# Second mixer with its differential branch first, bias loads spread over the experts, and one tile split ahead of the group copies

## The chip, the cores and the metric

The program runs on one core of one Trainium2 chip, in one launch. The metric is the device time of that core in microseconds (us). The core's engines run side by side and meet at semaphores: TensorE (PE, matmuls), VectorE (DVE), ScalarE (ACT), GpSimd (POOL) and SyncE (SP), which issues the weight loads.

## The reference

A sequence of 256 tokens of width 1024 passes two blocks in float32, each of two layers. The first block has a hybrid mixer and 32 experts, of which each token takes two out of one group of eight. The second block, which the larger part of the change is in, has per layer one input projection, four attention branches side by side, an output projection and an MLP:

```python
h = rms_norm_2(x, norm1_g[l])
proj = h @ w_in[l]                                   # 256 x 2400
(a_cq, a_ckv, a_kr, b_q, b_k, b_v, c_q, c_k, c_v, d_q, d_k, d_v) = jnp.split(proj, splits, axis=-1)
y_a = mla_mixer(...)    # A: latent; q = rms(cq) @ w_uq, k = rms(ckv) @ w_uk, v = rms(ckv) @ w_uv, rope, 4 heads
y_b = diff_mixer(...)   # B: differential; 4 heads x 2 softmaxes, w = p0 - lam * p1, rope
y_c = swa_mixer(...)    # C: sliding window with sinks, rope
y_d = na_mixer(...)     # D: neighbourhood, with the bias table na_rpb added to the scores
mix = jnp.concatenate([rms_norm_2(y_a, out_g_mla[l]), y_b, rms_norm_2(y_c, ...), rms_norm_2(y_d, ...)], axis=-1)
x = x + mix @ w_out[l]
h = rms_norm_2(x, norm2_g[l])
x = x + jnp.square(jax.nn.relu(h @ w_up[l])) @ w_down[l]
```

## The kernel before

**Weights.** Every weight matrix is cut into tiles of at most 1 MB (128 x 2048 float32). `tile()` lists them in one order, and SP loads them in that order into a ring of four slots. A slot is free when the tile four places back has been consumed. For nearly all tiles this means split: ACT writes the rounded high part of the tile into one of three `spl` buffers (`act_hi`, L356), DVE writes the rest (`dve_lo`, L365), and TensorE multiplies high and low parts in three passes. SP waits for the DVE part of the tile four back (`slot_free`). One tile per layer of the second block, the latent weights `("mla", l)`, is not split: TensorE reads it out of the ring, and its slot comes free only when the last of its matmuls (w_uv, L1666) is done.

**Experts** (`act_moe`, `dve_moe`, `pe_moe`, 32 per layer). Expert e brings three tiles, gate, up and down. TensorE does gate and up of e (L1112, 48 matmuls), down of e-1 (L1126, 12), and a turn (L1136). ACT does the silu (L1188), a copy (L1197) and three tile splits per expert. After each eight experts (a group) DVE scales the group's sum (L1300), ACT copies it (L1205), POOL and DVE finish it, and TensorE scatters it (L1148). In layer 1, at expert 12, ACT also issues eight small DMAs for the bias of branch D (`act_na_bias`, L1809).

**Second mixer** (`pe_mix2`, `act_mix2`, `dve_mix2`, `pool_mix2`). The input projection is six column blocks, n = 0 to 5, whose columns `IN2` lists. Its results go to four PSUM banks in turn (`in2_bank`). Attention is cut into 20 units, `UNITS` (4 of A, 8 of B, 4 of C, 4 of D), dealt out to three lanes, each with a bank of its own. A unit is three TensorE steps, scores (L1608), transposes of the probabilities (L1617) and the product with v (L1623), with a softmax by DVE and ACT between the first two and a copy by ACT (L1747) between the last two. `pe_misc2` and its counterparts hold the latent prologue (L1639 to L1666), the rope permutations and the end of each branch (`fin2`: a norm, transposes L1697, yT). The output projection (L1588) takes one tile of w_out per branch, in the order A, B, C, D, in two halves each, and adds all in PSUM.

**Order.** Each engine runs its instructions in the order written. In the mixer it is set by strings of digits, `ORDER`: 0 is the projections and splits, 1 to 3 the lanes, 4 the prologue and ends, 5 the eviction of the projection. `steps` takes one step of the lane that each digit names. Nothing moves at run time: an engine whose next instruction waits stands still, with all that is behind it.

## Time and profile before

| | |
|---|---|
| runs | 1802.02, 1809.95, 1810.55 us, median 1809.95 |
| profiled execution | 1809.67 us, of which the profile's span is 1807.4 us |
| busy, share of the span | PE 91%, DVE 65%, ACT 51%, POOL 4% |
| chain that ended last | PE 77%, DVE 10%, ACT 6%, DMA 5% |
| experts of layer 0 and of layer 1, TensorE's first gate matmul to the last down matmul | 284 to 573 us, 794 to 1098 us |
| second mixer, first projection matmul to the last output tile | 1107.7 to 1262.6 us, 1454.3 to 1609.8 us |
| MLP after it | to 1444 us, to the end |

The stage bounds are read from where L1112, L1126, L1560 and L1588 start and end in the timeline. Busy time is the sum of an engine's instructions. A wait in brackets in a row stands in front of its instruction and names what ended it.

### The profile page before, as it was taken

What the parts mean: (1) busy time and instruction counts of PE and PEld (TensorE: products, weight loads), DVE (VectorE), ACT (ScalarE), POOL (GpSimd) and SP (SyncE); (2) the same over time, 40 slices, a digit from 0 to 9 for tenths busy, and PEclk for the clock granted to TensorE, in tenths of its full rate; (3) what the DMA queues carried; (4) which work ended last, traced back from release to release, by engine and by line L of the source; (5) the groups of instructions that cost most, each with busy time, mean ns of one, the idle gap of its engine ahead of it and who ended that gap; (6) DMA issues with size and microseconds to landing.
All of it is one profiled execution on the core that took longest, in us unless ns stands there. A gap on an engine that the chain in (4) does not pass through costs nothing.

```text
span 1807.4 us, 24692 instructions
## 1 busy us (share of the span) xinstructions
PE 1651.7 (91%) x10344; PEld 1417.6 (78%) x10344; DVE 1169.6 (65%) x1311; ACT 922.3 (51%) x1128; POOL 80.5 (4%) x68
## 2 busy tenths in 40 slices
PE   4999868999998999679979998998999999989997
PEld 2676658988987687579878898786899878769996
DVE  1545466988997545759868897584555457645554
ACT  2443136777776453357757775453544445444442
POOL 0110000000000100000000002100000030000000
PEclk8999878999998999889989999996999999889999
DMA  9757244999987765229888994531456516315551
GB/s 344 273 216 261 99 175 147 372 345 347 369 340 271 279 226 201 99 73 374 344 275 332 342 360 122 169 117 62 146 189 205 171 42 195 103 47 190 191 195 65
DMA packets 132241, 392.06 MB, mean 217 GB/s; under 512 B 23200, under 2 KB 36384, under 8 KB 107552
## 3 DMA queue, kind: packets, MB, share of 16 engines
q1 hardware_dynamic: 125008, 386.11, 59.9%
q10 hardware_dynamic: 7120, 4.33, 1.0%
q8 instruction: 84, 1.38, 0.3%
q14 instruction: 29, 0.24, 0.0%
HBM read 389.37 MB, written 1.05 MB: 216 GB/s over the span
## 4 chain that ended last, share of the span: by engine, by line
PE 77%; DVE 10%; ACT 6%; DMA 5%; issue 1%; ACTq 1%; SPq 1%; POOL 0%; POOLq 0%; DVEq 0%
PE ps L1112 15%; PE ps L458 11%; PE ps L2057 10%; PE ps L1126 8%; PE ps L438 5%; DVE spl L365 4%; PE ps L1560 4%; ACT spl L356 3%; PE ps L1588 3%; PE ps L1608 2%; PE ps L500 2%; PE ps L1623 2%; DMA ring<-in_w_ada 2%; PE ps L1538 2%; PE ps L517 1%; PE ps L622 1%
## 5 line engine op out<-in xcount | busy, mean ns | idle before, releaser
L365 DVE TENSOR_TENSOR spl<-ring,spl 128x2048 fp32r<-128x2048 f32 (+2 forms) x318 | 722.0, 2274 | 275.5 <-ACT spl L356 274.4
L356 ACT ACTIVATE spl<-ring 128x2048 fp32r<-128x2048 f32 (+2 forms) x318 | 602.5, 1897 | 306.5 <-PE ps L458 105.3
L1112 PE MATMUL ps<-spl,ur 128*128 128x256 f32 x3072 | 373.6, 282 | 12.1 <-DVE spl L365 11.2
L1112 PEld LDWEIGHTS ps<-spl,ur 128*128 128x128 f32 x3072 | 362.7, 192 | 12.7 <-DVE spl L365 11.5
L458 PE MATMUL ps<-hh,spl 128*128 128x256 f32 x1728 | 207.9, 282 | 2.8 <-DVE hh L421 2.8
L458 PEld LDWEIGHTS ps<-hh,spl 128*128 128x128 f32 x1728 | 205.6, 190 | 5.7 <-issue 4.7
L1126 PE MATMUL ps<-spl,hh 128*128 128x512 f32 x768 | 187.6, 393 | 12.3 <-DVE spl L365 10.3
L2057 PE MATMUL ps<-spl,ur 128*128 128x512 f32 x768 | 176.7, 390 | 0.0
L1126 PEld LDWEIGHTS ps<-spl,hh 128*128 128x128 f32 x768 | 140.2, 188 | 42.3 <-DVE spl L365 12.9
L2057 PEld LDWEIGHTS ps<-spl,ur 128*128 128x128 f32 x768 | 143.2, 188 | 29.1
L438 PE MATMUL ps<-spl,hh 128*128 128x512 f32 x480 | 128.9, 423 | 0.1
L438 PEld LDWEIGHTS ps<-spl,hh 128*128 128x128 f32 x480 | 93.7, 200 | 37.4 <-issue 17.3
L1560 PE MATMUL ps<-hh,spl 128*128 128x256 f32 (+1 forms) x672 | 83.4, 282 | 0.3 <-DVE hh L421 0.3
L1560 PEld LDWEIGHTS ps<-hh,spl 128*128 128x128 f32 (+1 forms) x672 | 79.2, 186 | 3.0 <-issue 2.9
L507 ACT ACTIVATE ar<-ps 128x512 f32<-128x512 f32 x24 | 14.3, 596 | 81.8 <-PE ps L500 81.4
L1197 ACT ACTIVATE hh<-ps 128x256 fp32r<-128x256 f32 x64 | 24.7, 385 | 60.8 <-PE ps L1136 60.8
L500 PE MATMUL ps<-ring,ccol 128*32 128x512 f32 x384 | 51.7, 637 | 3.3 <-DMA ring<-in_w_ada 3.3
L379 ACT ACTIVATE xn<-x 128x512 f32<-128x512 f32 x36 | 22.6, 628 | 54.9 <-DVE x L2119 20.1
L375 POOL TENSOR_TENSOR st<-st 128x1 f32<-128x1 f32 x14 | 10.5, 747 | 835.9 <-DVE st L384 835.9
L1188 ACT ACTIVATE ar<-ps 128x256 f32<-128x256 f32 x64 | 24.4, 381 | 43.2 <-PE ps L1112 43.1
L396 PE MATMUL ps<-cst,xn 128*128 128x128 f32 x64 | 14.7, 423 | 34.4 <-DVE xn L390 34.4
L1608 PE MATMUL ps<-ar 64*128 64x256 f32 (+1 forms) x160 | 44.8, 451 | 0.0
(351 smaller groups left out, 1738.2 us busy)
## 6 DMA issues: line engine op xcount, KB each, us to landing
ring<-in_w_up SPq DMA_DIRECT2D x96, 1024.0 KB, 5.5
ring<-in_w_down SPq DMA_DIRECT2D x96, 1024.0 KB, 5.3
ring<-in_w_gate SPq DMA_DIRECT2D x64, 1024.0 KB, 5.1
ring<-in_w_ada SPq DMA_DIRECT2D x48, 1024.0 KB, 7.3
ring<-in_w_in SPq DMA_DIRECT2D x34, 1024.0 KB, 6.4
ring<-in_w_out SPq DMA_DIRECT2D x16, 1024.0 KB, 5.1
ring<-in_w_in SPq DMA_DIRECT2D x8, 384.0 KB, 4.3
gate<-in_b_ada ACTq DMA_DIRECT2D x4, 512.0 KB, 6.0
```

Source lines behind the costliest of these rows:

```text
L356: sc.activation(t.hi, t.raw, ACT.Copy).then_inc(s_hi, 1)
L365: v.tensor_tensor(t.lo, t.raw, t.hi, ALU.subtract).then_inc(s_lo, 1)
L438: ins = pe.matmul(ps[:, banks[i], 0:cn], le, ri, start=(kk == 0 and q == 0), stop=(kk == 7 and q == 2), skip_group_check=True)
L458: ins = pe.matmul(ps[:, banks[m // 2], (m % 2) * 256:(m % 2) * 256 + 256], le, ri, start=(kk == 0 and q == 0 and m % 2 == 0), stop=(kk == ...
L500: ins = pe.matmul(ps[32 * k:32 * k + 32, bank, :], ccol[:, 4 * half + k, :], t.raw[:, k, :], start=(half == 0), stop=(half == 1), skip_gro ...
L1112: ins = pe.matmul(ps[:, 2 + q, 256 * z:256 * z + 256], le, ri, start=(k == 0 and j == 0 and z == 0), stop=(k == 7 and j == 2), skip_group_ ...
L1126: ins = pe.matmul(ps[:, c, :], le, ri, start=(d % 8 == 0 and f == 0 and j == 0), stop=(d % 8 == 7 and f == 1 and j == 2), skip_group_check ...
L1538: ins = pe.matmul(o, le, ri, start=(kk == 0 and q == 0), stop=(kk == 7 and q == 2), skip_group_check=True)
L1560: ins = pe.matmul(o, le, ri, start=(kk == 0 and q == 0 and m % 2 == 0), stop=(kk == 7 and q == 2), skip_group_check=True)
L1588: ins = pe.matmul(ps[:, 2 * c + i, :], le, ri, start=(k == 0 and q == 0), stop=(k == 7 and q == 2), skip_group_check=True)
L1608: ins = pe.matmul(ps[:, L.b, 256 * j:256 * j + 256], q, k, start=True, stop=True)
L2057: ins = pe.matmul(ps[:, 2 * cc + i, :], le, ri, start=(d == 0 and f2 == 0 and f == 0 and q == 0), stop=(d == 7 and f2 == 1 and f == 1 and ...
```

## The change

1. In the second mixer the blocks are loaded and projected in the order B's q and k, B's and C's v, the latent columns, then the rest as before. `UNITS` begins with B. The projection's results rotate over three banks (0 to 2), the lanes move to banks 3 to 5, and the latent prologue has banks 6 and 7. The tile `("mla", l)` is loaded after the latent columns. The tiles of w_out are taken in the order B, A, C, D. The `ORDER` strings of the mixer are new, and three buffers move.
2. `act_na_bias` takes one load at a time. In layer 1's experts one is issued at experts 3, 5, 6, 11, 13, 14, 19 and 21; for the second mixer layer two at each of four steps of the MLP, not eight at one.
3. At the end of a group of experts ACT splits the next tile before it waits for the group's sum, not after the copies.

The arithmetic is the same.

```diff
+OUT2 = (1, 0, 2, 3)
-         ("mix2", 0, "PE"): "40000004004440440412312012301230101231042021404130123023012013012302131210231212132312142330423023030400",
+         ("mix2", 0, "PE"): "40000404000012300120123014230104123412020413041231232112042303043043012301321241230310123124210123023400",
...
-        IN2 = [[(0, 192), (320, 32), (192, 128)], [(352, 512)], [(864, 256), (1504, 128)], ...]
+        IN2 = [[(352, 512)], [(864, 256), (1504, 128)], [(0, 192), (320, 32), (192, 128)], ...]
...
-                if n == 0:
+                if n == 2:
                     uq = a["mla_w_uq_2"][l]
                     tile(("mla", l), [uq[0:128, :], uq[128:192, :], a["mla_w_uk_2"][l], a["mla_w_uv_2"][l]], split=False)
...
-                tile(("out2", l, t), [wo[:, 2 * t:2 * t + 2, :]], 2, 1024)
+                tile(("out2", l, t), [wo[:, 2 * OUT2[t]:2 * OUT2[t] + 2, :]], 2, 1024)
...
-                    if e == 12 and l == 1:
-                        act_na_bias(sc, 0)
+                    if l == 1 and e % 8 in (3, 5, 6):
+                        n = 3 * (e // 8) + (3, 5, 6).index(e % 8)
+                        if n < 8:
+                            act_na_bias(sc, 0, n)
                     act_hi(sc, last)
...
                 if e and e % 8 == 0:
+                    act_hi(sc, last)
                     gr = e // 8 - 1
...
-                if e:
+                elif e:
                     act_hi(sc, last)
...
-        m2.R, m2.R2 = carve(7168, 256), carve(7424, 2, 256)
+        m2.R, m2.R2 = carve(7168, 256), carve(10496, 2, 256)
...
-        m2.kz = [m2.kd, carve(8192, 2, 256)]
+        m2.kz = [m2.kd, gate[:, :, 768:1024]]
...
-        UNITS = [Unit(br, i, p) for br, n in (("A", 2), ("B", 4), ("C", 2), ("D", 2)) for p in range(n) for i in range(2)]
+        UNITS = [Unit(br, i, p) for br, n in (("B", 4), ("A", 2), ("C", 2), ("D", 2)) for p in range(n) for i in range(2)]
...
-                self.b, self.units = 4 + z, UNITS[z::3]
+                self.b, self.units = 3 + z, UNITS[z::3]
...
+        OB = (0, 1, 2, 6)
+
         def in2_bank(n, j):
-            return (2 * n + j) % 4
+            return (2 * n + j) % 3
+
+        in2_free = [((0, 0), (0, 0)), ((0, 0), (1, 1)), ((2, 2), (0, 3)), ((3, 0), (0, 4)), ((0, 5), (4, 6)), ((5, 7), (0, 8))]
...
-                pe.wait_ge(v_ms, 20 * l + (10, 16, 18, 20)[t])
+                pe.wait_ge(v_ms, 20 * l + (11, 16, 18, 20)[t])
...
-                o = ps[0:96, 4 + h // 2, 256 * (h % 2):256 * (h % 2) + 256]
+                o = ps[0:96, 6 + h // 2, 256 * (h % 2):256 * (h % 2) + 256]
...
-                if c == 4 and l == 0:
-                    act_na_bias(sc, 1)
+                if l == 0 and 1 <= c < 5:
+                    act_na_bias(sc, 1, 2 * c - 2)
+                    act_na_bias(sc, 1, 2 * c - 1)
```

In the rows below, a row is a line of the kernel, the operation, what it writes and reads, and the semaphores it waits for; the line numbers after the change are up to some 25 higher. First ACT at the end of the first group of experts (L1205 or L1209 the group's copies, L356 or L357 a tile split, L1188 or L1189 the silu, L1197 or L1200 the copy before it). Before:

```order
L356 ACTIVATE spl<-ring 128x2048 [waits split_tile_used,tile_landed0]
L1197 ACTIVATE hh<-ps 128x256 [waits split_tile_used,gated_T]
L1205 ACTIVATE hh<-ar 128x512 [waits group_gated] x2
L356 ACTIVATE spl<-ring 128x2048 [waits split_tile_used,tile_landed1]
L356 ACTIVATE spl<-ring 128x2048 [waits split_tile_used,tile_landed2]
L1188 ACTIVATE ar<-ps 128x256 [waits gated,split_tile_used]
```

After:

```order
L357 ACTIVATE spl<-ring 128x2048 [waits split_tile_used,tile_landed0]
L1200 ACTIVATE hh<-ps 128x256 [waits split_tile_used,gated_T]
L357 ACTIVATE spl<-ring 128x2048 [waits split_tile_used,tile_landed1]
L1209 ACTIVATE hh<-ar 128x512 [waits group_gated] x2
L357 ACTIVATE spl<-ring 128x2048 [waits split_tile_used,tile_landed2]
L1189 ACTIVATE ar<-ps 128x256 [waits gated,split_tile_used]
```

The copies, which wait for the group's sum, and the split of the next tile have changed places.

Next ACT in the mixer, where it splits the tile whose ring slot the latent weights held (the L356 and L357 of slot 0, `tile_landed0`). L1766 and L1788 evict latent q, L1741 and L1756 are exponentials of a unit, L1747 and L1762 copy transposed probabilities, L1803 and L1805 belong to the end of branch B. Before:

```order
L1766 ACTIVATE ar<-ps 96x1024 [waits mix2_psum]
L1769 ACTIVATE ar<-ps 64x1024 [waits mix2_psum]
L1771 ACTIVATE st<-st 128x2 [waits lambda_sums]
L356 ACTIVATE spl<-ring 128x1536 [waits split_tile_used,tile_landed0]
L356 ACTIVATE spl<-ring 128x1536 [waits split_tile_used,tile_landed1]
L1741 ACTIVATE xn,st<-ps,st 128x256 [waits mix2_unit0_vector]
L1741 ACTIVATE xn,st<-ps,st 128x256
```

After:

```order
L1762 ACTIVATE xn<-ps 128x256 [waits mix2_unit0_psum]
L1762 ACTIVATE ar<-ps 128x256 [waits mix2_unit2_psum]
L1762 ACTIVATE xn<-ps 128x256 [waits mix2_unit1_psum]
L1756 ACTIVATE xn,st<-ps,st 128x256 [waits mix2_unit0_vector]
L1756 ACTIVATE xn,st<-ps,st 128x256
L357 ACTIVATE spl<-ring 128x2048 [waits split_tile_used,tile_landed0]
L1803 ACTIVATE st<-st 128x8 [waits mix2_vector]
L1805 ACTIVATE st<-st 128x8 [waits scalar_own]
L1762 ACTIVATE xn<-ps 128x512 [waits mix2_unit0_psum]
```

Before, the exponentials of three units stood behind that split; now the end of branch B and the copy of lane 0 do, in the midst of the units.

Last, TensorE in the mixer after the last block of the projection (L1588 or L1601 half a tile of the output projection, 12 matmuls; the others are scores, transposes and products of units). Before:

```order
L1588 MATMUL ps<-spl,ur 128x512 x12
L1617 MATMUL ps<-cst,xn 128x128 [waits mix2_unit1_scalar]
L1617 MATMUL ps<-cst,xn 128x128 x3
L1617 MATMUL ps<-cst,ar 128x128 [waits mix2_unit2_vector]
L1617 MATMUL ps<-cst,ar 128x128
L1617 MATMUL ps<-cst,xn 128x128 [waits mix2_unit0_scalar]
L1617 MATMUL ps<-cst,xn 128x128 x3
L1623 MATMUL ps<-ar,xn 128x64 [waits mix2_unit1_scalar]
L1623 MATMUL ps<-ar,xn 128x64 x3
L1623 MATMUL ps<-ar,xn 128x64 [waits mix2_unit0_scalar]
L1623 MATMUL ps<-ar,xn 128x64 x3
L1608 MATMUL ps<-ar 128x256 [waits in2_vector,in2_scalar,mix2_scalar,mix2_vector,mix2_unit1_vector]
```

After:

```order
L1631 MATMUL ps<-cst,ar 128x128 [waits mix2_unit2_scalar]
L1631 MATMUL ps<-cst,ar 128x128 x3
L1601 MATMUL ps<-spl,ur 128x512 [waits mix2_vector,tile_lo]
L1601 MATMUL ps<-spl,ur 128x512 x11
L1637 MATMUL ps<-ar 128x64 [waits mix2_unit2_scalar]
L1637 MATMUL ps<-ar 128x64 x3
L1631 MATMUL ps<-cst,xn 128x128 [waits mix2_unit0_scalar]
L1631 MATMUL ps<-cst,xn 128x128 x3
L1601 MATMUL ps<-spl,ur 128x512 x12
L1637 MATMUL ps<-ar,xn 128x64 [waits mix2_unit0_scalar]
L1637 MATMUL ps<-ar,xn 128x64 x3
L1631 MATMUL ps<-cst,xn 128x128 [waits mix2_unit1_scalar]
```

Before, the second half of the first output tile was followed by 34 rows of unit steps until the next one. Now the halves of the tiles of B, A and C stand singly between a few steps of the units.

## Rows read from the trace of the kernel before

**Rows 1.** Windows: length, then busy of PE, PEld, DVE, ACT, POOL; PEclk, DMA share, GB/s
```profile
371.00:442.00 71.00, 69.63 (x504) 65.01 (x504) 63.78 (x47) 51.11 (x43) 2.55 (x2) 1.00 0.94 356
900.00:930.00 30.00, 19.02 (x123) 17.90 (x122) 15.12 (x10) 11.85 (x11) 0.00 (x0) 0.77 0.82 257
...
1107.70:1262.60 154.90, 142.15 (x844) 119.11 (x844) 100.68 (x196) 73.48 (x167) 14.36 (x9) 0.89 0.33 102
1454.30:1609.80 155.50, 142.53 (x845) 119.28 (x845) 100.52 (x196) 73.42 (x167) 14.41 (x9) 0.90 0.33 102
1564.00:1588.50 24.50, 22.40 (x84) 18.27 (x84) 12.56 (x34) 9.47 (x31) 0.00 (x0) 0.50 0.14 43
```

**Rows 2.** Waits in the experts of layer 0: total us, times, longest
```profile
PE ps L1126 <- DVE spl L365: 5.1, 3, 1.7
```

**Rows 3.** Waits in the experts of layer 1
```profile
PE ps L1112 <- DVE spl L365: 11.2, 2, 11.0
...
PE ps L1126 <- DVE spl L365: 5.2, 3, 1.8
```

**Rows 4.** Timeline at the end of the first group: start us, us, what, idle before
```profile
365.60 1.23 ACT L1205 ACTIVATE hh<-ar 128x512 fp32r<-128x512 f32 x2 [2.11 <-DVE ar L1300]
...
366.73 3.70 ACT L356 ACTIVATE spl<-ring 128x2048 fp32r<-128x2048 f32 x2
...
368.35 1.09 PE L1148 MATMUL ps<-hh 128*128 128x512 f32 x4
368.67 4.54 DVE L365 TENSOR_TENSOR spl<-ring,spl 128x2048 fp32r<-128x2048 f32 x2 [2.51 <-ACT spl L356]
...
371.06 3.03 PE L1126 MATMUL ps<-spl,hh 128*128 128x512 f32 x12 [1.61 <-DVE spl L365]
```

**Rows 5.** Timeline at expert 12 of layer 1
```profile
906.42 12.26 ACTq L1809 DMA_DIRECT2D ar<-in_na_rpb  x8
...
923.07 5.49 PE L1112 MATMUL ps<-spl,ur 128*128 128x256 f32 x24 [10.98 <-DVE spl L365]
```

**Rows 6.** The line of the bias loads, all 16: ns min/median/max
```profile
L1809 ACTq DMA_DIRECT2D ar<-in_na_rpb x16: 618/673/2877, 906.4 to 1373.0; - x16
```

**Rows 7.** Timeline of a steady expert of layer 0: tile "up"
```profile
351.96 1.91 ACT L356 ACTIVATE spl<-ring 128x2048 fp32r<-128x2048 f32 x1
...
353.90 2.29 DVE L365 TENSOR_TENSOR spl<-ring,spl 128x2048 fp32r<-128x2048 f32 x1 [0.24 <-ACT spl L356]
...
354.38 5.70 PE L1112 MATMUL ps<-spl,ur 128*128 128x256 f32 x48
```

**Rows 8.** Weight loads, issue to landing: 380 to 440 us, then 960 to 1000 us
```profile
DMA to landing us min/median/max: 4.7/5.5/6.5
...
DMA to landing us min/median/max: 4.9/7.2/7.6
```

**Rows 9.** DMA queues of the page: packets, MB, share of 16 engines
```profile
q1 hardware_dynamic: 125008, 386.11, 59.9%
q10 hardware_dynamic: 7120, 4.33, 1.0%
```

**Rows 10.** TensorE's waits in the second mixer layer, 1454 to 1610 us
```profile
PE ps L1617 <- ACT xn L1741: 5.6, 4, 3.4
PE ps L1588 <- DVE hh L1992: 4.7, 1, 4.7
PE ps L1617 <- DVE ar L1904: 1.5, 1, 1.5
```

**Rows 11.** Timeline, scores (L1608): the first, later ones at full and at half clock
```profile
1492.22 2.76 PE L1608 MATMUL ps<-ar 96*128 96x256 f32 x12
...
1554.18 1.13 PE L1608 MATMUL ps<-ar 64*128 64x256 f32 x4
...
1574.33 2.07 PE L1608 MATMUL ps<-ar 64*128 64x256 f32 x4
```

**Rows 12.** Lines by form, second mixer layer: eviction of a projection block by ACT
```profile
L1718 ACT ACTIVATE ar<-ps 128x512 f32<-128x512 f32 x3 | 1.8, 607 | 3.6 <-PE ps L1560 3.6
```

More of the change, by code:

```diff
@@ L1553, in pe_in2 @@
                 for m, (cols, o) in enumerate(chunks):
+                    if half == 0 and m % 2 == 0:
+                        free(m // 2)
                     for k in range(4):
@@ L1627, in pe_misc2 @@
         def pe_misc2(pe, l):
-            P, A, V = 13 * l, 13 * l, 20 * l
+            A, V = 13 * l, 20 * l
+            r = slice(64, 96)
             pe.wait_ge(s_dg, l + 1)
@@ L1668, in pe_misc2 @@
             yield
[L1669 to L1677 removed]
+            yield from pe_fin2(pe, l, "B", V + 10)
+            pe.wait_ge(v_ms, V + 11)
             for z in range(2):
```

220 lines of the change are left out of this document (112 added, 108 removed), and 4 rows, old and new, of the table ORDER.

## The prediction

> **What bounds the kernel now.** I read the windows by stage first, then TensorE's waits in each stage, then the timeline around the longest of them, then the DMA queues. In a steady stretch of experts TensorE is busy 69.63 of 71.00 us, at a clock of 1.00 [rows 1]; DVE follows with 63.8 and the DMA engines' share is 0.94. So the experts are bound by TensorE, with DMA close behind: whatever TensorE stops waiting for there is time won, unless weights then come late. The second mixer is different: busy 142.5 of 155.5 us, DMA share 0.33, mean clock 0.90 [rows 1]. It has waits to lose (13.0 us) and a slow stretch: in 24.5 us from 1564 the granted clock is 0.50, the lower of its two levels (1.2 of 2.4 GHz). Four score matmuls take 2.07 us there and 1.13 just before [rows 11]. All that I add up belongs to the profiled execution, 1809.67 us (span 1807.4), which stands 0.3 below the runs' median; the runs spread over 8.5 us, and 0.5%, 9 us, is about what a measurement can tell from no change.
>
> **Part 3, the split ahead of the group copies.** At a group's end ACT has nothing to do for 2.11 us before 365.60, because its copies wait for DVE's sum; only then come two tile splits, 3.70 us for both [rows 4]. DVE stands idle 2.51 us for the first (from 366.16), and TensorE 1.61 us for DVE. The change puts one split, 1.85 us, into ACT's idle 2.11: it runs from 363.5 to 365.3 and the copies lose nothing. DVE can begin its half at 366.16, takes 2.27, and ends at 368.4, while TensorE scatters until 369.44. So the whole wait in front of L1126 goes, and the copies' end, 366.8, is early enough for the scatter at 368.35, where it was before. The split tiles after it come no later than before, since ACT has the same work in a row. The waits of this kind are 5.1 us in layer 0 and 5.2 in layer 1, three each [rows 2, 3]. Nothing is added. Saved: **10.3**. What is late next is the load: TensorE asks for weights 1.7 us sooner at each boundary, with a DMA share of 0.94 that is possible only because the ring had the same 1.7 us to fill. Bounds: 0 to 10.3.
>
> **Part 2, the bias loads.** At expert 12 ACT issues eight loads in 12.26 us [rows 5], behind which its silu stands; DVE and then TensorE stop, 10.98 us, the largest single wait of the kernel; it is the 11.0 in [rows 3]. Eight times the median 0.673 [rows 6] would be 5.4, and the longest is 2.88: part of the 12.26 is waiting of one issue for those ahead of it. After it the clock is 0.77 over 30 us [rows 1], loads land in 7.2 us instead of 5.5 [rows 8], and I count about 1.5 us of small waits. Saved: **11.0** and something of that 1.5.
> Spread, one load costs ACT 0.67 us. It stands where a tile split follows: ACT's split at 351.96 takes 1.91, DVE's half ends at 356.19, and TensorE, 24 of whose 48 matmuls take 2.75 us, needs that tile at 357.13 (354.38 + 2.75) [rows 7]. The slack is 0.94 us and a load of the median length fits. If each took 2.88 us, 1.9 of it would show, eight times: 15.5. I take the median, since the long ones stood in one burst behind each other.
> The bytes do not vanish either. The weights' queue moved 386 MB in 59.9% of the span, the queue that carries the bias 4.33 MB in 1.0% [rows 9]; by 1807.4 us that is 2.8 and 4.2 us of all 16 engines for a MB. The 0.2 MB of one load then costs at least 0.55 us; if the dear part of that queue is the bias, some 0.65. In experts with 0.94 of the DMA time taken, eight of these are at most 5.2 us if DMA is the bound, nothing if the ring absorbs them. One load gets some 20 us to be absorbed, in which 0.06 × 20 = 1.2 us is free: I take **+1.0** in all. The eight loads of the second mixer layer now stand in four pairs in the MLP; before, the one block of them stopped nothing there; 0.
> The Trainium skill, DMA: Bandwidth & Descriptors, section "Why small descriptors are slow (HBM only)", speaks against spreading small rows into a full pipe: a 256-byte descriptor costs 11 cycles where its bytes need 8. As an estimate by that page a load would cost 0.2 MB × 2.8 × 27% more, near 0.8 us, close to the row's own 0.55 to 0.65; no sum changes by it, only the chance of the fourth rival.
>
> **Part 1, the mixer.** Its time is 142.5 busy and 13.0 of waits. The waits: 5.6 for the exponentials of units (longest 3.4), 4.7 for the last y of branch D before the last output tile, 1.5 for DVE, the rest small [rows 10].
> First the clock. In the slow stretch (22.4 us busy) each operation takes 2.07/1.13 as long or nearly [rows 11]; 22.4 × (1 − 1.13/2.07) = 10.2 us are lost. Before it the order has 34 rows of unit steps without an output half between them, with waits in between, the 1.5 of [rows 10] the first. After the change the halves of three output tiles stand in the midst of them, so TensorE has dense work between its waits. The row shows that the clock fell behind small matmuls and waits; what I conclude, that it will not fall, or less, is a judgement and not a row. Bounds: 0 and 10.2 in a layer.
> Then the start. Branch A needs a long prologue: its first scores stand at 1492.22, 37.9 us after the first projection matmul (1454.3) [rows 11], and the longest wait, 3.4, is behind them, when there is no other unit ready. B has only its rope: ahead of its first scores the new order has 120 projection matmuls 256 wide and 48 that are 384 wide, which in the timeline of this stage take 1.4 and 2.2 us a dozen, and 1.3 us of rope: 14.1 + 8.8 + 1.3, 24 us. That wait for exponentials goes, as more of the projection lies between the steps. But the order has one new wait. The latent weights are loaded one block later and hold their ring slot until w_uv; the tile four behind them is loaded only then, and needs 5.5 us to land, 1.9 for ACT and 2.3 for DVE, 9.7 in all [rows 7, 8], against some 6.6 us of TensorE's work that stands in the order between w_uv and the tile's first matmul. That is 3 us, and ACT's split of it stands in front of lane 0's copy and the end of B. With this 3, the 4.7 at the end (branch D is still last) and 5 for small waits, about as many as now, I have 12.7 against 13.0 of waits: no gain there. So the mixer is 142.5 − 10.2 + 12.7 = 145.0, by 10.5 shorter. Since the clock could fall for a short while all the same, I take **9.5** in a layer, two layers, 19.0. Against it, in the first layer the first tile is 2048 wide and not 1408, with the last group of experts ahead of it: DVE's half takes 0.7 us more before the last sum, of which I count **+0.5**.
> Three banks instead of four for the projection: a bank's eviction by ACT takes 0.61 us [rows 12] and the bank comes round after two others, of which 12 matmuls each take 1.4 us or more (DVE's evictions, 0.7 for the 512 columns, no longer). This costs 0. The skill's Perfetto Trace Analysis, section "Matmuls", says that independent groups should rotate through banks so that the eviction overlaps; fewer banks would cost by it up to one eviction per bank turn. By the row it is covered.
>
> **Sum.** −10.3 − 11.0 + 1.0 − 19.0 + 0.5 = −38.8; 1809.7 − 38.8 = 1770.9, **1771**. Own range 1764 to 1779.
>
> **Rivals.**
> (R2) The mixer gains little: the clock falls again somewhere, since scores and transposes are as many as before, or the slot's wait eats what the clock gives. For it: both layers have the same mean clock [rows 1], and the new order keeps a wait of 3 us. Against it: dense halves between them. Time: 1809.7 − 20.3 + 0.5 = 1790 (10.3 + 11.0 − 1.0 saved). Chance 0.22.
> (R3) All goes well: the clock stays full in both mixers, the small waits shrink too (5 less in each layer), the loads cost nothing: 1771 − 1 − 2 × 5 − 1.5 = 1758 or 1759. Chance 0.14.
> (R4) DMA becomes the bound of the experts: boundaries and loads bring TensorE ahead of the ring, and of part 3 half comes back as waits for landings, 5.2, and the loads cost 5.2 and not 1.0: 1771 + 5.2 + 4.2 = 1780. For it: share 0.94, landing 7.2 where the ring was pressed. Against it: an expert needs 8.44 us by TensorE and 0.94 of it by DMA. Chance 0.12.
> (R5) Slower. The tile behind the latent weights comes so late that ACT, standing at its split, holds the copies and exponentials of all three lanes, and TensorE runs dry. Parts 2 and 3 give 20.3, so each mixer must lose 10 us, and the tile must be 20.6 us later than in my walk, 24 us late in all; the longest landing of [rows 8] is 7.6. With 4 us more, for the copies that stand behind it, it is 1771 + 2 × (20.6 + 4) = 1820. Chance 0.03.
> That the change does not do what it says: the order shows all three moved, so only the clock is in doubt, which is R2.
>
> **Chances.** Forecast 0.49, R2 0.22, R3 0.14, R4 0.12, R5 0.03. Faster by over 0.5% (under 1801): all of the first four except a part of R2 in which the mixer loses 10 us and more, 0.05; so 0.92, same 0.05, slower 0.03. The range 1757 to 1791 takes in R2's and R3's centres and leaves out 0.17: R5 and about a third of R2 and R3 each, beyond their centres.
>
> **What would show it.** In the experts the three waits of the down matmuls (L1126) for DVE's half go in each layer, and no wait of 11 us stands in layer 1; landings stay under 6.5 us. In layer 1 TensorE's waits around experts 3, 5, 6 and so on are below 0.5 us each; if they are 1 us or more, ACT's issue is longer than 0.67. In the mixer the first scores come 24 us after the start; the granted clock is 1.00 in every slice behind the projection; a wait of 2 to 4 us stands before a projection block after w_uv, for DVE's split half; and from first matmul to last output tile it is 145 to 147 us. The prediction is wrong if the mixers have a stretch at 0.50 again, if the wait for that tile is 8 us or more, or if the experts' span shrinks by under 15 us in layer 1.

## The result, and the profile after

The changed kernel takes 1795.56 us (median of 6 runs, 1789.53 to 1800.85), the kernel before 1809.0 us (6 runs, 1802.02 to 1819.48). The ratio is 0.9918, 95% interval 0.9893 to 0.9943. It is faster, clear of the noise and as forecast, but by 13 us and not by 39, and it lies outside the range of 1757 to 1791.

The table gives the span stage by stage, read from the starts of rows in the timeline of TensorE: experts from the first gate matmul to the last down matmul, mixers from the first projection matmul to the last output tile. The fourth column is the difference of the two profiled executions (1809.67 and 1800.85 us), the last one the prediction's.

| stage, us | before | after | difference | forecast |
|---|---|---|---|---|
| up to the first expert | 284.3 | 288.5 | +4.2 | 0 |
| experts, layer 0 | 285.3 | 283.9 | −1.5 | −5.1 |
| from there to the experts of layer 1 | 223.9 | 225.2 | +1.3 | 0 |
| experts, layer 1 | 301.2 | 300.6 | −0.5 | −15.2 |
| to the second mixer | 13.0 | 13.6 | +0.6 | +0.5 |
| second mixer, layer 0 | 155.0 | 149.0 | −6.0 | −9.5 |
| last tile and MLP | 191.7 | 191.8 | +0.2 | 0 |
| second mixer, layer 1 | 155.5 | 149.5 | −6.0 | −9.5 |
| last tile, MLP, end | 197.6 | 196.7 | −1.0 | 0 |

The change does not touch what lies ahead of the first expert; over the runs of this study that stretch took from 281 to 290 us whatever the kernel, so its 4.2 us are chance. Without them the profile has 13 us, as the medians have. The gain is nearly all in the mixers. Of the two mixers only the second is a firm measure. The mixer of layer 1 took 155.5 to 155.7 us in the three profiles in which its code is that of before, and 149.4 to 149.5 in those in which it is that of the changed kernel. The mixer of layer 0 took 151.6, 151.6 and 155.0 us with the code of before and 145.0 to 150.4 with the changed one, so that a part of its 6.0 us can be chance. The experts of layer 1, which were to give 15 us, gave half of one.

First the waits of TensorE in the experts of layer 0 (total us, times, longest), which answer to [rows 2]:

```profile
PE ps L1149 <- POOL hh L1338: 3.6, 3, 1.6
...
PE ps L1137 <- DVE ar L1290: 2.1, 1, 2.1
```

The wait for the split before L1127 (L1126 before) is gone, as the step said. In its place the scatter L1149 waits for POOL, three times, 3.6 us. The timeline at the end of the first group shows why; it answers to [rows 4]:

```profile
369.85 1.23 ACT L1209 ACTIVATE hh<-ar 128x512 fp32r<-128x512 f32 x2 [0.30 <-DVE ar L1304]
370.34 2.28 DVE L366 TENSOR_TENSOR spl<-ring,spl 128x2048 fp32r<-128x2048 f32 x1
370.57 6.47 POOL L1338 TENSOR_TENSOR hh<-ar,hh 128x512 fp32r<-128x512 f32 x2 [116.14 <-ACT hh L1209]
...
372.93 2.97 DVE L366 TENSOR_TENSOR spl<-ring,spl 128x2048 fp32r<-128x2048 f32 x1 [0.31 <-ACT spl L357]
```

ACT's copies now stand 0.3 us behind DVE's sum, and DVE splits the tile at 370.34, where before it was idle. In that time POOL does the group's two subtractions, in 6.47 us. The next split of DVE is longer too, 2.97 us where one of this size otherwise takes 2.29. In the same view of the kernel before, at the same place, POOL needed 2.55 for the two, in the time in which DVE stood idle:

```profile
366.31 2.55 POOL L1334 TENSOR_TENSOR hh<-ar,hh 128x512 fp32r<-128x512 f32 x2 [116.16 <-ACT hh L1205]
```

Next the same waits in the experts of layer 1, which answer to [rows 3]:

```profile
PE ps L1137 <- DVE ar L1290: 6.2, 6, 2.3
PE ps L1113 <- DVE spl L366: 5.6, 4, 2.9
PE ps L1149 <- POOL hh L1338: 4.0, 3, 1.6
...
PE ps L1127 <- DVE spl L366: 0.4, 1, 0.4
```

The stall of 11.0 is gone. But L1113 waits four times for a split, 5.6 us, and the turn L1137 six times, 6.2. The kernel before waited 2.9 there, by the same view:

```profile
PE ps L1136 <- DVE ar L1286: 2.9, 3, 2.0
```

The timeline around the first bias load (start, duration, what, in brackets the wait ahead of it):

```profile
830.78 0.70 ACTq L1828 DMA_DIRECT2D ar<-in_na_rpb  x1
...
843.52 1.92 ACT L357 ACTIVATE spl<-ring 128x2048 fp32r<-128x2048 f32 x1 [3.93 <-DMA ring<-in_w_up]
...
847.82 3.49 PE L1113 MATMUL ps<-spl,ur 128*128 128x256 f32 x15 [2.92 <-DVE spl L366]
```

The issue on ACT is 0.70 us, as priced. What was not priced stands below it: until 12.7 us later ACT has waited 3.93 us for the landing of a weight tile, TensorE 2.92 for its split, and then the clock is down for a while, so that 15 matmuls take 3.49 us. The landings of the weight loads in the 18 us ahead of this load and in the 18 behind it:

```profile
DMA to landing us min/median/max: 4.7/5.1/5.7
...
DMA to landing us min/median/max: 4.8/9.9/11.1
```

And a window of 8 us behind it (columns as in [rows 1]); 228 GB/s moved where the steady experts had 356 (a window that begins and ends 1 us later has 274):

```profile
834.00:842.00 8.00, 8.00 (x61) 7.51 (x60) 7.05 (x5) 4.25 (x4) 0.00 (x0) 1.00 0.87 228
```

Last the mixer. Windows of the steady experts, of both mixers and of three slow stretches in the second of them (the first with 22 matmuls in 6 us), as in [rows 1]:

```profile
371.00:442.00 71.00, 69.98 (x509) 65.50 (x508) 65.79 (x47) 51.79 (x44) 6.70 (x3) 1.00 0.94 358
1111.76:1260.71 148.95, 136.14 (x844) 115.17 (x845) 100.69 (x193) 72.53 (x165) 13.86 (x9) 0.92 0.34 110
1452.55:1602.05 149.50, 136.68 (x845) 115.74 (x845) 100.55 (x193) 72.53 (x165) 13.92 (x9) 0.92 0.34 110
1506.00:1512.00 6.00, 6.00 (x22) 4.36 (x21) 2.81 (x4) 2.00 (x8) 4.69 (x4) 0.54 0.00 0
1531.00:1536.00 5.00, 4.72 (x22) 4.72 (x23) 3.83 (x7) 5.00 (x12) 0.00 (x0) 0.50 1.03 409
1584.00:1589.00 5.00, 5.00 (x16) 4.06 (x16) 2.07 (x7) 2.37 (x9) 0.00 (x0) 0.56 0.03 9
```

Against [rows 1] TensorE is busy 6.0 and 5.9 us less, and what is left beside it, the waits, is 12.8 us in each, as before. The clock is at or near its lower level in three short stretches; before, it was there in the one of 24.5 us and for some 3 us near 1500, right behind the wait of 3.4 in [rows 10] (0.50 from 1500 to 1502). The waits in the mixer of layer 1, answering to [rows 10]:

```profile
PE ps L1637 <- ACT xn L1762: 5.2, 3, 3.4
PE ps L1712 <- DVE gate L2003: 3.3, 1, 3.3
PE ps L1601 <- DVE hh L2008: 1.9, 1, 1.9
PE ps L1601 <- DVE ur L2008: 1.3, 1, 1.3
PE ps L1622 <- DVE gate L1931: 1.0, 1, 1.0
```

The longest of them, the slow operations behind it, and the end of the mixer:

```profile
1531.28 1.97 PE L1637 MATMUL ps<-ar,xn 128*128 128x64 f32 x8 [3.35 <-ACT xn L1762]
...
1533.75 4.58 PE L1577 MATMUL ps<-hh,spl 128*128 128x256 f32 x24
...
1599.03 1.08 PE L1712 MATMUL ps<-cst,gate 128*128 128x128 f32 x4 [3.35 <-DVE gate L2003]
1602.05 7.31 PE L1601 MATMUL ps<-spl,hh 128*128 128x512 f32 x24 [1.93 <-DVE hh L2008]
```

The 24 matmuls of the projection take 4.58 us there, at full clock 2.98. And ACT in front of the first of these waits:

```profile
1528.40 1.91 ACT L357 ACTIVATE spl<-ring 128x2048 fp32r<-128x2048 f32 x1 [1.19 <-DMA ring<-in_w_in]
...
1530.65 0.58 ACT L1762 ACTIVATE xn<-ps 128x512 f32<-128x512 f32 x1
```

This is the ring-slot tile that the prediction walked: ACT splits it at 1528.40 (it waited 1.2 us for the landing), and lane 0's copy, for which TensorE waits, stands behind it until 1530.65.

### The profile page after: what moved, and what is told of

It is laid out like the page before. It is cut to its first block, busy times and chain, and to the rows that moved or that the text cites. A ratio compares the mean times of both kernels' runs of the same rounds, so it can differ in the third digit from the quotient of the medians.

```text
span 1798.7 us, 24694 instructions
## 1 busy us (share of the span) xinstructions
PE 1647.3 (92%) x10344; PEld 1412.5 (79%) x10344; DVE 1179.5 (66%) x1311; ACT 924.9 (51%) x1128; POOL 101.3 (6%) x68
## 3 DMA queue, kind: packets, MB, share of 16 engines
q10 hardware_dynamic: 7120, 4.33, 1.2%
## 4 chain that ended last, share of the span: by engine, by line
PE 73%; DVE 11%; DMA 8%; ACT 6%; POOL 1%; issue 1%; SPq 0%; DVEq 0%; ACTq 0%; POOLq 0%
PE ps L1113 13%; PE ps L459 11%; PE ps L2077 10%; PE ps L1127 6%; PE ps L439 6%; DVE spl L366 5%; PE ps L1577 5%; ACT spl L357 4%; DMA ring<-in_w_up 3%; PE ps L1601 2%; PE ps L501 2%; DMA ring<-in_w_ada 2%; PE ps L1553 2%; PE ps L518 1%; PE ps L1637 1%; PE ps L623 1%
## 5 line engine op out<-in xcount | busy, mean ns | idle before, releaser
L366 DVE TENSOR_TENSOR spl<-ring,spl 128x2048 fp32r<-128x2048 f32 (+2 forms) x318 | 730.5, 2299 | 275.5 <-ACT spl L357 274.1
L357 ACT ACTIVATE spl<-ring 128x2048 fp32r<-128x2048 f32 (+2 forms) x318 | 603.7, 1899 | 310.3 <-PE ps L459 108.0
L1113 PE MATMUL ps<-spl,ur 128*128 128x256 f32 x3072 | 375.2, 282 | 6.5 <-DVE spl L366 5.6
L1113 PEld LDWEIGHTS ps<-spl,ur 128*128 128x128 f32 x3072 | 363.9, 192 | 7.5 <-DVE spl L366 6.4
L1127 PE MATMUL ps<-spl,hh 128*128 128x512 f32 x768 | 186.8, 392 | 2.6 <-DVE hh L1298 2.0
L1127 PEld LDWEIGHTS ps<-spl,hh 128*128 128x128 f32 x768 | 140.4, 188 | 30.6 <-issue 2.4
L1577 PE MATMUL ps<-hh,spl 128*128 128x256 f32 (+1 forms) x672 | 88.9, 292 | 1.2 <-DVE hh L422 1.2
L1577 PEld LDWEIGHTS ps<-hh,spl 128*128 128x128 f32 (+1 forms) x672 | 84.8, 198 | 2.9 <-issue 2.9
L1338 POOL TENSOR_TENSOR hh<-ar,hh 128x512 fp32r<-128x512 f32 x12 | 38.1, 3190 | 507.0 <-ACT hh L1209 507.0
L1200 ACT ACTIVATE hh<-ps 128x256 fp32r<-128x256 f32 x64 | 24.5, 383 | 60.3 <-PE ps L1137 60.1
L1189 ACT ACTIVATE ar<-ps 128x256 f32<-128x256 f32 x64 | 24.4, 381 | 40.3 <-PE ps L1113 40.3
```

Of the source, the lines that this page charges most:

```text
L357: sc.activation(t.hi, t.raw, ACT.Copy).then_inc(s_hi, 1)
L366: v.tensor_tensor(t.lo, t.raw, t.hi, ALU.subtract).then_inc(s_lo, 1)
L1113: ins = pe.matmul(ps[:, 2 + q, 256 * z:256 * z + 256], le, ri, start=(k == 0 and j == 0 and z == 0), stop=(k == 7 and j == 2), skip_group_ ...
L1127: ins = pe.matmul(ps[:, c, :], le, ri, start=(d % 8 == 0 and f == 0 and j == 0), stop=(d % 8 == 7 and f == 1 and j == 2), skip_group_check ...
L1338: po.tensor_tensor(mo.ys[1][:, h], mo.yg[:, h], mo.ys[0][:, h], ALU.subtract).then_inc(s_y1, 1)
L1577: ins = pe.matmul(o, le, ri, start=(kk == 0 and q == 0 and m % 2 == 0), stop=(kk == 7 and q == 2), skip_group_check=True)
```

## Experiments

Each part was first put alone into the kernel before, side by side on one chip (kernel before there 1812.09 us, 17 runs). Stage times and rows are of one profile for each kernel. Profiles of the same experts' code differ: with the changed kernel's code the experts of layer 1 took 300.6, 303.1 and 298.7 us, those of layer 0 282.8 to 283.9.

### Part 3 alone

```diff
@@ act_moe, kernel before
                 if e and e % 8 == 0:
+                    act_hi(sc, last)
...
-                if e:
+                elif e:
                     act_hi(sc, last)
```

> The kernel before with part 3 alone (the split of the next tile ahead of the group copies). Theory 1, GpSimd and VectorE get in each other's way: before, the group's subtraction on POOL ran while DVE stood idle (1.3 us each); with DVE at its half of the tile at the same time it takes about 3.2 us each, and TensorE's scatter waits for POOL instead of for the split, 1.0 to 1.6 us per group. Then the six waits of 10.3 us in all turn into about 7.5 us of waits for POOL, and the kernel gains 3 us or less (1806 to 1807). Theory 2, weights come late: POOL stays at 1.3 us, the wait for the split goes, and ACT waits for landings in the experts behind a boundary, with the same small gain. The prediction's own sum: 10.3 us, 1799.

1803.84 us (7 runs), ratio 0.9957 (0.9940 to 0.9973). The experts take 282.8 us in layer 0 and 295.6 in layer 1 (before 285.3 and 301.2); the stage between them is 1.3 us longer, as in the changed kernel. POOL's subtractions in layer 0, as a line of the costliest groups (count, busy us, mean ns, idle before):

```profile
L1335 POOL TENSOR_TENSOR hh<-ar,hh 128x512 fp32r<-128x512 f32 x6 | 19.2, 3222 | 243.4 <-ACT hh L1206 243.4
```

And TensorE's wait for them:

```profile
PE ps L1148 <- POOL hh L1335: 3.1, 3, 1.0
```

The first theory holds in its mechanism: 3.2 us each, and 3.1 us of waits for POOL in place of 5.1 for the split. In the experts of layer 0 ACT waits for no landing, which speaks against the second theory. The size is open. The runs' medians give 8.3 us, more than the 3 that the expectation had at most; the stages up to the second mixer give 5 us net, about half of the 10.3: 8.1 in the experts, less 3.1 given back behind them.

### Part 2 alone

```diff
@@ act_moe and act_mlp, kernel before
-                    if e == 12 and l == 1:
-                        act_na_bias(sc, 0)
+                    if l == 1 and e % 8 in (3, 5, 6):
+                        n = 3 * (e // 8) + (3, 5, 6).index(e % 8)
+                        if n < 8:
+                            act_na_bias(sc, 0, n)
```

> The kernel before with part 2 alone (bias loads one at a time in the experts of layer 1, and in pairs in the MLP). Theory 1: each load, 384 rows of 256 bytes, slows the weights' queue for some 8 us, so that weights land in up to 11 us where they took 5, and ACT waits for them; the eight loads cost 8 to 10 us in all in place of the one stall of 11, and the gain is 1 to 3 us (1806 to 1808). Theory 2: the loads are hidden, and what held the changed kernel back in these experts was its earlier boundaries; then 10 us are gained here, 1799. The issue on ACT, 0.6 us each, shows in neither.

1812.08 us (10 runs), ratio 0.9995 (0.9979 to 1.0011): no gain at all. The experts of layer 1 take 300.8 us. Their waits:

```profile
PE ps L1112 <- DVE spl L365: 10.6, 6, 2.8
PE ps L1126 <- DVE spl L365: 5.2, 3, 1.8
```

The boundaries are as before here, so they are not what makes the weights late: the loads alone turn the one stall of 11.0 into six waits of 10.6. That is the first theory, though its 1 to 3 us of gain did not show.

### Part 1 alone

```diff
@@ changed kernel: the experts and the MLP as before, the mixer as changed
-                    if l == 1 and e % 8 in (3, 5, 6):
...
+                    if e == 12 and l == 1:
+                        act_na_bias(sc, 0)
...
-                elif e:
+                if e:
                     act_hi(sc, last)
```

> Part 1 alone: the changed kernel with the experts' and the MLP's part as before. If the stages are independent, each mixer takes 149 to 149.5 us from its first projection matmul to its last output tile, 6.0 less than before, and the kernel 12 us less, 1797; the stall of 11 us at expert 12 is back. If the mixer's clock depended on what comes ahead of it, its slow stretches lie elsewhere, and the gain is between 5 and 20 us.

1799.88 us (5 runs), ratio 0.9932 (0.9904 to 0.9959), 12 us less. The mixers take 150.4 and 149.4 us. So the mixer's part alone gives about what the whole change gave. Alone the three parts gave 8.3, 0 and 12.2 us, 20.5 in sum, and together 13.4. The intervals are wide, but the profiles have 5 us of this at one place: the experts of layer 1 take 295.6 us with the early split and the loads in one burst, and 300.6 with the early split and the loads spread.

### The loads of the first mixer layer moved out of the experts

```diff
@@ changed kernel
-                    if l == 1 and e % 8 in (3, 5, 6):
...
@@ act_misc2: ahead of the squares, the norm factors, latent q and latent k
+            load(0)
             sc.wait_ge(v_ev, 10 * l + 5)
...
+            load(6)
             sc.wait_ge(p_ms, P + 7)
```

> The changed kernel with the eight loads for mixer layer 0 taken out of the experts and issued in pairs at four steps of that mixer (the squares, the norm factors, latent q, latent k), where its DMA queues stand idle. Theory 1 (the loads slow the weights): the experts of layer 1 lose the waits for landings, 8 to 9 us, and take 291 to 293 us from the first gate matmul to the last down in place of 300.6; the mixer is unchanged within 0.5 us; the kernel comes to 1787. Theory 2 (the earlier boundaries bring TensorE ahead of the ring): the experts keep most of these waits, over 5 us. Rival: the bias comes too late for the mask on POOL and for the units of branch D, and the mixer is longer by 2 us or more.

1778.13 us (4 runs), ratio to before 0.9815 (0.9792 to 0.9838); 17 us less than the changed kernel (on another chip), the largest step of this study. The experts of layer 1 take 282.9 us, shorter by 17.7, where the first theory had expected 8 to 9; the mixers are as before this edit (149.5 and 149.5). The wait for a split tile is gone; the largest of the waits inside these experts is

```profile
PE ps L1149 <- POOL hh L1334: 3.1, 3, 1.0
```

The landings of the weight loads from 830 to 1070 us (in the changed kernel the median of that stretch is 7.2):

```profile
DMA to landing us min/median/max: 4.7/5.1/6.7
```

The boundaries are as early here as in the changed kernel, and the loads land in 5.1 us. The second theory, that the earlier boundaries outrun the ring, falls. Eight loads of 98 KB cost 17.7 us when spread; in one burst, by the kernel with part 3 alone (295.6), 12.7.

### What in a load is dear: the rows, or the bytes

```diff
@@ act_na_bias, layer 0 only; narrow rows
-  ... [[1, 64], [31, 6], [1, 64]])
+  ... [[1, 64], [31, 6], [1, 4]])
@@ act_na_bias, layer 0 only; long rows
-  ... [[1, 64], [31, 6], [1, 64]])
+  ... [[1, 64], [1, 384]])
```

> The changed kernel, but the eight loads of layer 0's bias move 4 of 64 columns: the same 384 rows each, of 16 bytes in place of 256 (so the bias of that layer is incomplete). Theory 1, the number of rows sets the price: weights land as late as before the edit and the experts of layer 1 stay at 299 to 301 us. Theory 2, the bytes set it: one sixteenth is left and these experts take 283 to 285 us, as with no load in them at all (282.9).

> The changed kernel, but each of the eight loads reads 64 contiguous rows of 1536 bytes in place of 384 of 256 bytes: the same bytes in a sixth of the rows (the bias of that layer has other values). Theory 1, the number of rows: the experts of layer 1 take 285 to 287 us, a sixth of the 17.7 left. Theory 2, the bytes: 299 to 301 us.

One profile each. Narrow rows: 291.8 us in the experts of layer 1, 8.8 above the 282.9 without loads. Long rows: 287.3, 4.3 above. With both, the number of rows and their bytes, it was 17.7. So neither theory is right: each alone costs a part, many rows of next to no bytes about half. The two parts sum to 13.1; that this is less than the whole is not sure, with profiles of the same code up to 4 us apart. ACT's waits for landings between 800 and 1080 us go the same way: none without loads in the experts, 17.1 us in all with long rows, 25.7 with narrow rows, 28.5 in the changed kernel. With the long rows TensorE never waits for a split tile, and its added waits stand at the turn (3.2 us for 1.9) and at the scatter (4.7 for 3.1).

### Three loads far apart

```diff
@@ changed kernel, loads in the mixer except three
+                    if l == 1 and e in (3, 11, 19):
+                        act_na_bias(sc, 0, 3 * (e // 8))
```

> The kernel with the loads moved into the mixer, but three of the eight left in the experts of layer 1, at experts 3, 11 and 19, 67 us from each other. Each alone: if the price of a load is a fixed one (17.7 us for eight, 2.2 each), these experts take 289 to 290 us; if the ring recovers between loads that stand far apart and only neighbours (experts 3, 5, 6) add up, 284 to 286 us; with no load it was 282.9.

296.7 us: three loads cost 13.7, more than either theory had. The gate and up matmuls behind each of them (24, which take 2.99 us at full clock):

```profile
839.59 4.49 PE L1113 MATMUL ps<-spl,ur 128*128 128x256 f32 x24 [3.03 <-DVE spl L366]
...
914.79 4.44 PE L1113 MATMUL ps<-spl,ur 128*128 128x256 f32 x24 [2.79 <-DVE spl L366]
...
990.07 4.32 PE L1113 MATMUL ps<-spl,ur 128*128 128x256 f32 x24 [2.92 <-DVE spl L366]
```

In this profile a load alone has one price, each time the same: 3 us of waiting and 1.4 us of half clock behind it, 4.5 in all. With eight loads it is less regular. The first of them is followed by a wait of 2.9, 3.8 and 1.2 us in the three profiles with the changed kernel's experts, the one at expert 11 by waits of 0.6 and 0.7 in the first of these. Those at experts 5 and 6 that follow another add little (eight cost 17.7 and not 36). This points away from an amount of DMA time, which would add up, and to the lateness of a tile: TensorE has a certain slack in its tiles, the first load uses it up, and the stall that it makes gives the slack back. This account is argued from the waits; no experiment changed the slack.

### GpSimd ahead of VectorE

```diff
@@ dve_moe, changed kernel
                     if gr == 3:
...
+                    else:
+                        v.wait_ge(s_y1, 8 * l + 2 * gr + 2)
                 if e:
                     dve_lo(v, last)
```

> The changed kernel, but VectorE waits at the end of a group until GpSimd has done its two subtractions, and only then takes its half of the tile. If the two engines get in each other's way (shared access), the subtractions go back from 3.2 to 1.3 us each, and TensorE's waits for POOL in front of the scatter go; waits for the tile's half come in their place, about 2 us later than now, so that the experts of layer 0 stay within 1.5 us of 283.8. If they do not, the subtraction stays at 3.2 us, and TensorE waits longer for both, 287 us or more.

The same two views, POOL's line and TensorE's wait, in layer 0:

```profile
L1340 POOL TENSOR_TENSOR hh<-ar,hh 128x512 fp32r<-128x512 f32 x6 | 7.7, 1298 | 254.6 <-ACT hh L1209 254.6
```

TensorE:

```profile
PE ps L1127 <- DVE spl L366: 5.6, 3, 1.9
```

The subtraction is back at 1.30 us, and only what DVE does beside it has changed. DVE's splits behind it take 2.29 us each, where in the changed kernel the two after the first took 2.97 and 2.98. The two engines slow each other there, that is shown. The starts in the changed kernel look as if they took turns: DVE's first split ends at 372.62, and the scatter that needs POOL's first subtraction starts 1.18 us later, at 373.80. This is a reading of one boundary and was not tested. The expectation's size was off: the experts take 287.2 us, since DVE waits for all of POOL's work and the wait for the split is 5.6.

### VectorE does the subtraction

```diff
@@ dve_moe and pool_moe, with the loads in the mixer
-                    if gr == 3:
+                    if True:
                         for c in range(2):
-                            v.wait_ge(s_y0, 8 * l + 7 + c)
+                            v.wait_ge(s_y0, 8 * l + 2 * gr + 1 + c)
...
-            for gr in range(3):
-                    po.tensor_tensor(mo.ys[1][:, h], mo.yg[:, h], mo.ys[0][:, h], ALU.subtract).then_inc(s_y1, 1)
```

> A version meant to beat both: the bias loads of mixer layer 0 issued in that mixer, and in addition the group's subtraction done by VectorE right behind ACT's copies, ahead of its half of the tile, for every group, not by GpSimd. Nothing runs on GpSimd there; a subtraction takes VectorE about 0.6 us where GpSimd takes 3.2 beside it. If the waits of 1.0 to 1.6 us for POOL go and VectorE is only 1.3 us later with the tile, which TensorE needs behind the scatter, each layer of experts gains up to 3.5 us on the kernel with the loads alone moved, 1771 to 1776; the rival is that VectorE, busy for 0.85 of the experts, passes its delay on to the next tile, and nothing is gained, 1778 to 1780.

1776.28 us (6 runs) beside 1808.24 for before on that chip, ratio 0.9809 (0.9784 to 0.9834). The experts take 281.5 and 281.2 us, 2.2 and 1.8 less than with the loads alone moved. The waits of layer 0:

```profile
PE ps L1127 <- DVE spl L366: 1.2, 3, 0.4
```

No wait for POOL, and 1.2 us for the split in three. Against the kernel with the loads alone moved the intervals overlap; only the stages tell the 4 us. In layer 0 they tell it firmly: 281.5 to 281.7 us in the three profiles with VectorE's subtraction, never under 282.8 in those with GpSimd's. It was run again beside the last kernel below:

> The same version without the extra matmuls, on the same chip, to compare the two: 1776 if the chips are alike, with 147 to 149.5 us in each mixer.

1774.28 us (5 runs), ratio 0.9804 (0.9782 to 0.9827), mixers 147.8 and 149.5.

### ACT's order at the ring-slot tile

```diff
@@ ORDER["mix2", l, "ACT"], both layers
-  "4005500501230120431421542315241 3210412 302043035..."
+  "4005500501230120431421542315241 3214102 302043035..."
```

> The changed kernel with ACT's split of the tile whose ring slot the latent weights held put behind the end of B and lane 0's copy, in both mixer layers. If that split causes the wait of 3.35 us ahead of lane 0's product, the wait falls to 1.3 us or less; the split tile comes 1 us later, so TensorE waits for it up to 1.5 us, and the mixer takes 147.5 to 149 us. Rival: the wait only moves in front of the projection block, with the same fall of the clock, and the mixer stays within 0.5 us of 149.5.

The mixer of layer 1 takes 149.33 us, so the rival holds. Its waits:

```profile
PE ps L1637 <- ACT xn L1762: 2.8, 3, 1.6
PE ps L1631 <- ACT xn L1756: 1.6, 1, 1.6
```

L1637's wait is 2.8 in all and not 5.2, but L1631 waits 1.6 where it waited for nothing, so part of the wait has only moved. The mixer of layer 0 took 147.3 us, within what the changed code took there in other profiles.

### Extra matmuls in the gaps

```diff
@@ pe_units, changed kernel
+                if u.br == "A" and L is LANES[0] and n == 3:
+                    for k in range(24):
+                        pe.matmul(ps[:, 7, 0:256], hT[0][:, k % 8, 0:128], hT[0][:, k % 8, :], start=True, stop=True)
                 pe.wait_ge(L.scalar, 2 * at + 2)
```

> The changed kernel with 24 extra matmuls, 256 wide, about 2.8 us, whose result nobody reads, where TensorE stands 3.35 us in the mixer (ahead of lane 0's product after the first unit of A). Theory 1, the gap makes the clock fall: the granted clock then stays at 1.00 in the 5 us behind it, and the mixer takes 146.5 to 147.5 us in place of 149.5, although it does more. Theory 2, the small matmuls ahead of the gap make it fall: the mixer stays at 149 to 150 us with a clock near 0.5 behind that place. Theory 3, the extra work is in the way: over 150 us.

The mixer of layer 1 takes 147.35 us, 2.15 less, with 3.1 us more of work. TensorE behind the filler (L1636), and, from the first mixer layer, the last output tile:

```profile
1528.50 3.12 PE L1636 MATMUL ps<-hh 128*128 128x256 f32 x24
1531.96 1.10 PE L1640 MATMUL ps<-ar,xn 128*128 128x64 f32 x8 [0.35 <-ACT xn L1765]
...
1533.38 3.10 PE L1577 MATMUL ps<-hh,spl 128*128 128x256 f32 x24
...
1258.41 8.49 PE L1601 MATMUL ps<-spl,hh 128*128 128x512 f32 x24 [1.93 <-DVE hh L2011]
```

The 24 projection matmuls behind the gap take 3.10 us; in the changed kernel they took 4.58. So the gap it was. But the last tile takes 8.49 us and not 7.31: 1.2 us of the gain is given back at the end, behind the next gaps. The whole kernel, run once, took 1799.61 us beside 1812.59 for before, no less than the changed kernel. So all three were filled, in the version with VectorE's subtraction:

```diff
@@ pe_misc2
             pe.wait_ge(v_ms, V + 18)
+            for k in range(24):
+                pe.matmul(ps[:, 7, 0:256], m2.yT[0][0][:, k % 4, 0:128], m2.yT[0][0][:, k % 4, :], start=True, stop=True)
             yield from pe_fin2(pe, l, "D", V + 19)
@@ pe_main2
+                if t == 3:
+                    for k in range(14):
+                        pe.matmul(ps[:, 3, 0:256], m2.yT[0][0][:, k % 4, 0:128], m2.yT[0][0][:, k % 4, :], start=True, stop=True)
                 pe.wait_ge(v_ms, 20 * l + (11, 16, 18, 20)[t])
```

> The version with the loads in the mixer and VectorE's subtraction (1776 beside 1808 us before), with extra matmuls whose result nobody reads in the three gaps of each mixer: 24 ahead of lane 0's product after the first unit of A (a wait of 3.35 us), 24 ahead of the turn of branch D (3.35) and 14 ahead of the last output tile (1.93). If each gap makes the granted clock fall behind it, the clock stays at 1.00 behind all three, the last tile takes 6.2 us in place of 7.3 to 8.5, and the mixer with its last tile is 3 to 4 us shorter per layer: 1768 to 1771. Rival: the slow stretch only comes later, or the extra work delays the waited-for step, and the kernel stays at 1775 to 1777.

1764.32 us (5 runs), against 1774.28 for the same without filler on the same chip and 1811.31 for before: ratio to before 0.9737 (0.9714 to 0.9760). The mixer of layer 1 as a window:

```profile
1418.72:1562.68 143.96, 138.81 (x907) 118.67 (x907) 100.86 (x193) 72.34 (x165) 13.92 (x9) 0.96 0.35 112
```

And its end in the timeline (L1701 and L1585 are filler):

```profile
1556.73 3.12 PE L1701 MATMUL ps<-ur 128*128 128x256 f32 x24
1560.18 0.66 PE L1709 MATMUL ps<-cst,gate 128*128 128x128 f32 x4 [0.33 <-DVE gate L2009]
1560.59 1.91 PE L1585 MATMUL ps<-ur 128*128 128x256 f32 x14
1562.68 5.74 PE L1593 MATMUL ps<-spl,hh 128*128 128x512 f32 x24 [0.17 <-DVE hh L2014]
```

The mean clock is 0.96 in place of 0.92, the mixers take 144.0 us each, and the last tile 5.74. This is 10 us less by the medians, and 5.5 us in the mixer of layer 1 where 3 to 4 were expected with its last tile. Two short stretches near half clock remain, one behind the latent matmuls, one behind the waits of 1.6 and 1.0 us, which were not filled. It is the fastest version here: 0.9737 of the kernel before, where the changed kernel has 0.9918.

## Why the prediction was wrong

**The bias loads: this step failed.** "One load gets some 20 us to be absorbed, in which 0.06 × 20 = 1.2 us is free: I take +1.0 in all." The runs: part 2 alone gains 0 ± 3 us in place of 10, and eight loads spread over the experts cost 17.7 us. The price was worked out as a share of DMA time, 0.65 us a load, averaged over 20 us. What the waits follow is how late one weight tile lands: 11.1 us for 5, against slack for about 3 of these 6 (the rest was TensorE's wait of 2.9), with a half-clock stretch behind it. The bounds were wrong for the same reason: "at most 5.2 us if DMA is the bound" took the loads' own DMA time as the most they could cost, and the profile had a sign that they cost more, the landing of 7.2 us in [rows 8] behind the burst. A slip of arithmetic stands beside it: a load is 98 KB, not "0.2 MB", so that "at least 0.55 us" is 0.28. The 0.65 us come out all the same if the rest of that queue's 4.33 MB is put at 2.8 us for a MB, which leaves 6.6 for the bias, an estimate; the +1.0 of the sum did not hang on it. The issue on ACT, 0.6 to 0.7 us within the slack, was right. The fourth rival had the mechanism, late landings, at 5.2 us and in the wrong company: it gave half of the blame to the earlier boundaries, and with the same boundaries and no loads ACT waited for no landing there. The Trainium skill, DMA: Bandwidth & Descriptors, section "Why small descriptors are slow (HBM only)", gives a 256-byte descriptor 11 cycles, 3 of them overhead, and calls this 27%. That is 27% of the 11; against the 8 cycles of the bytes it is 11/8. As an estimate by that page a load of 98 KB takes 0.098 × 2.8 × 11/8 = 0.38 us, not the 0.8 of the prediction. The trace had 6 us of lateness behind one load, so a price of this size does not explain it.

**The boundaries: right wait, wrong cover.** The six waits of 10.3 us went, to the 0.4 that is left in layer 1. "Nothing is added" was wrong: POOL's subtraction, which ran in DVE's idle 2.5 us, now runs beside DVE's split, takes 3.2 us for 1.3, and the scatter waits 3.6 and 4.0 us for it. The prediction counted ACT, DVE and TensorE at the boundary and left out the fourth engine, whose row stands at 366.31 in the timeline of before. The stage behind the experts of layer 0 gave another 1.3 back; its cause stays open. With part 3 alone it was in all 5 us by stages, 8.3 by the medians.

**The mixer: waits right, clock mis-sized. This step failed too.** The waits were forecast at 12.7 us, and the rows above sum to 12.7 (12.8 by the windows) with the one of 3.35 behind the ring-slot tile, forecast at 3. That wait stands in front of lane 0's product, behind ACT's copy, and not, as the prediction had it, in front of a projection block for DVE's half. The first scores stand 24.3 us after the start, forecast 24. The gain in the clock was put at 10.2 (9.5 taken with a margin), and TensorE's busy time fell by 5.9 to 6.0. The term "10.2 us" assumed that dense work between the units keeps the clock up throughout; three stretches of 5 to 6 us remain, one behind latent matmuls of few columns without any wait ahead, two behind waits of 3.35 and of 1.6 and 1.0 us. The trace of the kernel before had a sign of this that the prediction passed over: the clock of 0.50 from 1500 to 1502, right behind a wait of 3.35 us, while the order kept a wait of 3 and the 4.7 at the end. Which of the two, small matmuls or waits, makes the clock fall, no row of the long stretch told. The filler does for the gaps: the stretch behind a filled gap goes. For the one behind the latent matmuls no cause was tested.

**What held.** The sign, the tile behind the large wait and its size, the issue cost, three banks at no cost (no wait for an eviction of the projection stands among the waits), and the MLP's loads at nothing (191.7 and 191.8 us). Faster by over 0.5%, at 0.92, came, with 0.8%. The range rested on a sum whose second largest term had been bounded too tightly; and R5 with a third of R2 and R3 leaves out 0.15, not the 0.17 of the prediction. Two of the prediction's own signs of being wrong came: stretches near 0.50 in the mixers, and an experts' span of layer 1 that shrank by 0.5 us and not by 15. A third misled: waits of 1 us and more behind the loads were to mean a longer issue on ACT, and the issue was as priced.

## What to carry to other kernels

A side transfer in a stretch where every tile is just in time was not paid by its share of bandwidth; the waits followed how late it made one tile. So put it where the queue is idle, even if it looks cheap. Spreading it did not pay here: beside the late boundaries it gave nothing (1812.08 and 1812.09 us), beside the early ones the burst was 5 us cheaper, in one profile each. When an idle time is filled on one engine, list every engine that worked in that idle time, the small ones too. Where a dense engine stands still for a few microseconds and its clock falls behind the gap, the gap costs more than its length.

## What was not expected of the hardware

- In the changed kernel a 98 KB load of 384 rows was followed by a 1 MB load, issued 1.6 us later, that landed after 11.1 us and not after about 5, and for 8 us the DMA engines move 228 GB/s where they moved 356. Without the small loads no landing there took over 6.7 us. The profile doesn't show which of the 16 engines or which part of the transfer holds it up, and that stays open.
- A subtraction of 128 x 512 on GpSimd takes 1.30 us with VectorE idle and 3.22 us with VectorE splitting a tile; VectorE's splits beside it take up to 2.98 us for 2.29.
- Matmuls without use, 62 in each mixer, make the kernel 10 us faster (1774.28 to 1764.32), and the clock, which fell to about half behind these gaps, does not fall there when they are filled.
